# Attention probabilities of sixteen heads: TensorE transposes replaced by 32x32 squares on VectorE and a round trip through DRAM

## What is computed

```python
D_MODEL, SEQ, N_HEADS = 1024, 256, 16        # moba: 16 heads of 64
FOX_HEADS = MLA_HEADS = 8                    # odd: 8 heads of 64, 8 of 96
def moba_attention(h, w_qkv, w_o):
    ...
    s_own = jnp.einsum('bhqd,bhjd->bhqj', qc, ko).astype(jnp.float32)
    s_own = jnp.where(kpos[None, :] <= qpos[:, None], s_own, NEG_INF)
    p = jax.nn.softmax(jnp.concatenate([s_sel, s_own], axis=-1), axis=-1).astype(v.dtype)
    ...
def block_causal_attention(q, k, v, log_decay_cum):
    ...
        sc = jnp.einsum('bhqd,bhkd->bhqk', qi, k).astype(F32) * scale
        if fi is not None:
            sc = sc + fi[..., :, None] - log_decay_cum[:, :, None, :]
        sc = jnp.where(kpos[None, :] <= qpos[:, None], sc, -jnp.inf)
        p = jax.nn.softmax(sc, axis=-1).astype(v.dtype)
        return jnp.einsum('bhqk,bhkd->bhqd', p, v)
```

## Time and profile before

| | |
|---|---|
| median of 3 runs | 1202.47 us (1202.43 to 1202.48) |
| span of the profiled execution | 1201.0 us |
| TensorE busy | 1191.7 us (99%) |
| VectorE busy | 881.1 us (73%) |
| ScalarE busy | 661.8 us (55%) |
| GpSimd busy | 52.7 us (4%) |
| DMA moved | 217.80 MB, mean 181 GB/s |

### The profile page before, as it was taken

One profiled execution on the slowest core, in us unless ns is written; L12 is line 12 of the kernel. 1 busy time (PEld: TensorE's weight loads), 2 busy tenths in 40 slices (PEclk: granted clock), 3 DMA queues, 4 the chain that ended last, 5 costly groups with the idle time before them and its releaser, 6 DMA issues.

```text
span 1201.0 us, 16544 instructions
## 1 busy us (share of the span) xinstructions
PE 1191.7 (99%) x6611; PEld 1025.8 (85%) x6611; DVE 881.1 (73%) x1227; ACT 661.8 (55%) x871; POOL 52.7 (4%) x75
## 2 busy tenths in 40 slices
PE   9999999999999999999999999999999999999997
PEld 8888888888777888888899888888889977888886
DVE  6977989847786798884688877776467667777744
ACT  6545666634566666663587645444337775544430
POOL 0000000000000000000005200000012001000000
PEclk9999999999999999999999999999999999999999
DMA  9755555564534555556434556555526433755530
GB/s 359 248 206 192 174 179 192 187 221 170 195 114 138 188 180 179 203 201 216 160 102 141 185 211 236 191 195 191 179 91 229 176 140 106 253 202 175 198 119 35
DMA packets 32652, 217.80 MB, mean 181 GB/s; under 512 B 3760, under 2 KB 4032, under 8 KB 8000
## 3 DMA queue, kind: packets, MB, share of 16 engines
q1 hardware_dynamic: 30704, 210.39, 49.5%
q0 software_dynamic: 1728, 6.29, 1.6%
q10 hardware_dynamic: 144, 0.07, 0.0%
HBM read 215.67 MB, written 1.05 MB: 180 GB/s over the span
## 4 chain that ended last, share of the span: by engine, by line
PE 99%; DVE 1%; DMA 0%; ACT 0%; issue 0%
PE ps L963 43%; PE ps L893 24%; PE ps L899 14%; PE ps L901 4%; PE ps L915 2%; PE ps L912 2%; PE ps L911 2%; PE ps L1004 1%; PE ps L977 1%; PE ps L1032 1%; PE ps L1014 1%; PE ps L1096 1%; DMA t<-in_cst 0%; PE ps L1042 0%; PE ps L1081 0%; PE ps L926 0%
## 5 line engine op out<-in xcount | busy, mean ns | idle before, releaser
L963 PE MATMUL ps<-t,t 128*128 128x512 f32 (+3 forms) x2328 | 538.4, 387 | 0.0
L1552 DVE TENSOR_TENSOR t<-t,t 128x2048 fp32r<-128x2048 f32 (+3 forms) x200 | 448.8, 2257 | 101.9 <-PE ps L963 87.7
L963 PEld LDWEIGHTS ps<-t,t 128*128 128x128 f32 x2328 | 423.1, 188 | 81.5 <-issue 1.8
L1205 ACT CAST t<-t 128x2048 fp32r<-128x2048 f32 (+3 forms) x200 | 374.6, 1883 | 202.3 <-PE ps L963 106.0
L893 PE MATMUL ps<-t,t 128*128 128x512 f32 x1274 | 305.8, 390 | 0.0
L893 PEld LDWEIGHTS ps<-t,t 128*128 128x128 f32 x1274 | 238.9, 188 | 51.2
L899 PEld LDWEIGHTS ps<-t,t 128*128 128x128 f32 x1456 | 187.2, 191 | 7.4
L899 PE MATMUL ps<-t,t 128*128 128x256 f32 x1456 | 189.5, 283 | 0.0
L1687 DVE TENSOR_REDUCE t<-ps 128x512 f32<-128x1024 f32 x40 | 49.0, 1225 | 44.3 <-PE ps L901 44.3
L1640 DVE SCALAR_TENSOR_TENSOR t<-t,t,t 128x254 f32<-128x254 f32 (+1 forms) x176 | 73.2, 478 | 10.2 <-ACT t L1230 10.2
L1270 ACT CAST t<-t 128x512 fp32r<-128x512 f32 x44 | 27.3, 620 | 91.2 <-DVE t L1671 91.2
(11 more groups left out here) (220 smaller groups left out, 846.0 us busy)
## 6 DMA issues: line engine op xcount, KB each, us to landing
t<-in_wts SPq DMA_DIRECT2D x192, 1024.0 KB, 4.9
t<-in_rows POOLq DMA_DIRECT2D x12, 512.0 KB, 4.4
t<-in_wts SPq DMA_DIRECT2D x4, 528.0 KB, 4.1
t<-in_wts SPq DMA_DIRECT2D x2, 768.0 KB, 4.8
t<-in_wts SPq DMA_DIRECT2D x2, 592.0 KB, 3.8
t<-in_x_in SPq DMA_DIRECT2D x2, 512.0 KB, 4.3
out<-t SPq DMA_DIRECT2D x4, 256.0 KB, 2.0
t<-in_wts SPq DMA_DIRECT2D x2, 256.0 KB, 6.3
```

Source lines behind the costliest of these rows:

```text
L963: ins = mm(ps[:, t_bank(stage, t, j), 0:c1 - c0], a, w[:, k, c0:c1], start=kt == 0 and part == 0, stop=kt == KTS[stage] - 1 and part == 2)
L1205: copy(wh[:, k, 0:w], wraw[:, r, 0:w]).then_inc(s_hi, 1)
L1552: tt(wl[:, k, 0:w], wraw[:, r, 0:w], wh[:, h, 0:w].bitcast(F32), ALU.subtract).then_inc(s_lo, 1)
```

## The change

For heads 0 to 7 of moba and the eight fox heads (16 to 23) the step `u` is gone. In its place:

- `d`: VectorE transposes the scaled probabilities in 32x32 squares (one instruction of 128x384, `STREAM_TRANSPOSE`) into one of two buffers, and SyncE writes that buffer to a scratch in DRAM (`spilled_probs`), 1536 bytes per partition.
- `r`: SyncE waits for the write's landing (for heads 4 and up in the attention also for the values of the head four before) and reads the scratch back in 4x128 pieces of 384 bytes, into the buffer that the values step takes.

A square transpose alone leaves a key's number in the wrong partition. For these heads the keys are therefore stored in spread order (key 4r+b at place 32b+r), by the copies that bring them from PSUM, so that the read back lands each key in its own partition. The mask and the row of forget sums follow that order. The turned probabilities now lie as (query block of 32, chunk, query) for all 32 heads, so the values matmuls read them, and write PSUM, in pieces. TensorE waits for the reads of all heads of a values step. SyncE issues a load at `+l` instead of `+h`. Two values steps move: `p3` by three token steps, `p19` one ahead.

```diff
-@q1 t0.0 n1 t0.1 t1.0 +h t1.1 t2.0 +l +l vcopy0 t2.1 u0 s2 n2 u1 t3.0 t3.1 t4.0 n3 t4.1 t5.0 u2 s4 t5.1 u3 t6.0 t6.1
-n4 +h +l +h t7.0 t7.1
-@k1 t0.0 s6 n5 rope1.1.0 p3 t0.1 u4 t1.0 t1.1 t2.0 t2.1 t3.0 t3.1 u5 t4.0 n6 t4.1 t5.0 t5.1 +h +l u6 t6.0 t6.1 t7.0
-t7.1 cross1.1.0
+@q1 t0.0 n1 d1 r0 t0.1 t1.0 +h t1.1 t2.0 r1 +l +l vcopy0 t2.1 s2 n2 d2 t3.0 t3.1 t4.0 n3 d3 r2 t4.1 t5.0 s4 t5.1 t6.0
+r3 t6.1 n4 d4 +h +l +h t7.0 t7.1
+@k1 t0.0 s6 n5 d5 rope1.1.0 t0.1 t1.0 t1.1 p3 r4 t2.0 r5 t2.1 t3.0 t3.1 t4.0 n6 d6 t4.1 t5.0 t5.1 r6 +h +l t6.0 t6.1
+t7.0 t7.1 cross1.1.0
...
-+l +l +l t5.1 t6.0 +h +h vfcopy t6.1 n18 n19 t7.0 t7.1 f2.0 +l +h u17 f2.1 +l +h u18 qcopy1 f3.0 f3.1
-@uq kcopy1 u19 t0.0 s20 t1.0 s21 n20 t2.0 n21 +h s22 s23 queries0 t3.0 t0.1 p19 u20 n22 t1.1 t2.1 +h t3.1
++l +l +l t5.1 t6.0 +h +h vfcopy t6.1 n18 d18 r17 n19 d19 t7.0 t7.1 f2.0 r18 +l +h f2.1 r19 +l +h qcopy1 f3.0 f3.1
+@uq kcopy1 t0.0 s20 t1.0 s21 n20 d20 t2.0 n21 d21 +h s22 s23 queries0 t3.0 p19 r20 t0.1 n22 d22 r21 t1.1 t2.1 +h t3.1
...
+        def turn_squares(a, h):
+
+            n = D_AT[16 * a + h]
+            if n > 2:
+                dve.wait_ge(s_spill[(n - 1) % 2], 16 * ((n - 1) // 2))
+            dve.wait_ge(s_pnorm, 16 * a + h + 1)
+            dst = squares_of(16 * a + h).rearrange("p (b c i) -> p c b i", b=4, c=3)
+            nc.vector.transpose(dst, ATT_MEM[a][0][:, h % 4, :].rearrange("p (c b i) -> p c b i", c=3, b=4)
+                                ).then_inc(s_square, 1)
...
-            if kind in ("pump", "pump_hi"):
+            if kind in ("pump", "pump_lo"):
...
+            elif kind == "d":
+                n = D_AT[k[0]]
+                sp.wait_ge(s_square, n)
+                dma(spill[n - 1], squares_of(k[0])).then_inc(s_spill[(n - 1) % 2], 16)
+            elif kind == "r":
+                a, h = k[0] // 16, k[0] % 16
+                n = D_AT[k[0]]
+                sp.wait_ge(*spilled(k[0]))
+                if h >= 4:
+                    sp.wait_ge(s_pv, valued_at(16 * a + h - 4))
+                dma(ATT_MEM[a][1][:, h % 4, :].rearrange("p (a f) -> p a f", a=4),
+                    spill[n - 1].rearrange("q f -> (q f)").rearrange("(a p f) -> p a f", a=4, p=128)
+                    ).then_inc(s_back[h % 4], 16)
...
-            pe.wait_ge(s_ptc, 16 * a + last + 1)
+            for i in range(first, last + 1):
+                way, n = probs_left(16 * a + i)
+                if way == "u":
+                    pe.wait_ge(s_ptc, n)
+                else:
+                    pe.wait_ge(*back(16 * a + i))
...
-                        ins = mm(ps[64 * (i % 2):64 * (i % 2) + 64, 7, n * S + q.start:n * S + q.stop],
-                                 value_of(a, i, kt), PT[:, i % 4, p], start=kt == 0, stop=kt == 1)
+                        o = ps[64 * (i % 2):64 * (i % 2) + 64, 7, n * S + q.start:n * S + q.stop]
+                        ins = mm(o.rearrange("p (c a i) -> p a c i", a=4, i=32), value_of(a, i, kt),
+                                 turned_probs(a, i)[:, :, c, :], start=kt == 0, stop=kt == 1)
...
+                if is_k:
+                    for i in range(4):
+                        ins = copy(spread_keys(kh[0:64, 4 * m + i, :]),
+                                   in_spread_order(s3[64 * (i % 2):64 * (i % 2) + 64, i // 2, :]))
+                    ins.then_inc(s_kc, 1)
+                    return
```

More of the change, by code:

```diff
@@ L115 @@
 for _name, _cols in (("uo", 256), ("gt", 128), ("mask", 256), ("rope", 128), ("rope2", 64), ("cnt", 64),
[L116 removed]
+                     ("ident", 128), ("gain", 8), ("spread_mask", 256)):
     CST[_name] = _n
@@ L317, in all_steps @@
     out += [("rows", 2)] + ffn_steps(0, 2)
-    out += [("rows", 3), ] + mixed_steps(MOBA, None, 3)
+    out += [("rows", 3), ("probs_mask", 1)] + mixed_steps(MOBA, None, 3)
     out += [("rows", 4)] + ffn_steps(1, 4)
@@ L321, in all_steps @@
     out += [("rows", 6)] + ffn_steps(2, 6)
-    out += mixed_steps(ODD, "odd", 7)
+    out += [("probs_mask", 3)] + mixed_steps(ODD, "odd", 7)
     out += [("rows", 8)] + ffn_steps(3, 8)
@@ L358, with probs_left @@
 VALUED = [s[1] for s in STEPS if s[0] == "p"]
+U_AT = {s[1]: n for s, n in counted("u").items()}
+D_AT = {s[1]: n for s, n in counted("d").items()}
+SPREAD = set(range(8)) | set(range(16, 24))
+def probs_left(h):
+    return ("d", D_AT[h]) if h in D_AT else ("u", U_AT[h])
 def valued_from(last):
@@ L437, in program @@
     brow = fixed.take([128, 1024])
-    cs = fixed.take([128, NCST])
+    cs = fixed.take([128, NFIX])
     vecs = fixed.take([128, NVEC])
@@ L518, in program @@
     fc, fc2 = early.take([8, S]), early.take([8, S])
+    odd_squares = area_at(area.at).take([128, 2, 384])
     vm, vf = area.take([128, 2, 512]), area.take([128, 2, 512])
@@ L561, in program @@
     s_oh, s_ol = sem("s_heads_hi"), sem("s_heads_lo")
+    s_smask, s_square = sem("s_spread_mask_loaded"), sem("s_probs_squares_turned")
+    s_spill = [sem("s_even_probs_spilled"), sem("s_odd_probs_spilled")]
+    s_back = [sem(f"s_probs{i}_back") for i in range(4)]
     s_pw, s_us, s_xtap = sem("s_pool_w_loaded"), sem("s_u_copied"), sem("s_x_tap")
@@ L826, in six_free @@
         if was[0] == "u":
-            return s_ptc, was[1] + 1
+            return s_ptc, U_AT[was[1]]
         return (s_ac, ACROSS_AT[was]) if a else (s_crossed, CROSS_AT[was])
@@ L846, in qk_of, with squares_of, turned_probs, spilled @@
         return (qmT if is_q else kmT)[:, h - 8, cols]
+    SPREAD_MASK = (moba_mask, odd_mask)
+    def squares_of(h):
+        return (moba_squares if h < 16 else odd_squares if h < 20 else late_squares)[:, D_AT[h] % 2, :]
+    def turned_probs(a, h):
+        return ATT_MEM[a][1][:, h % 4, :].rearrange("p (a c i) -> p a c i", a=4, c=3)
+    def spilled(h):
+        n = D_AT[h]
+        return s_spill[(n - 1) % 2], 16 * ((n + 1) // 2)
+    def back(h):
+        return s_back[h % 4], 16 * sum(d <= h and d % 4 == h % 4 for d in D_AT)
+    def in_spread_order(ap):
+        return ap.rearrange("p (n r b) -> p n b r", r=32, b=4)
+    def spread_keys(ap):
+        return ap.rearrange("p (n b r) -> p n b r", b=4, r=32)
     def att_scale(a, h):
@@ L1017, in values @@
         def values(a, last):
-            PT, first = ATT_MEM[a][1], valued_from(16 * a + last) - 16 * a
+            first = valued_from(16 * a + last) - 16 * a
             if first:
@@ L1295, in copy_cross @@
                 copy(qT[:, i1:i1 + 2, :], s3).then_inc(s_crossed, 1)
+            elif 2 * i1 in SPREAD:
+                keys = kT[:, i1:i1 + 2, :].rearrange("p a s -> p (a s)")
+                copy(spread_keys(keys), in_spread_order(ps[:, 6, :])).then_inc(s_crossed, 1)
             else:
@@ L1422, in odd_step @@
                 act.wait_ge(s_t, T_AT["t", "ukv", 1, t])
+                for h in (18, 19):
+                    act.wait_ge(*spilled(h))
                 b2 = ps[:, 2 * t:2 * t + 2, :]
@@ L1431, in odd_step @@
                 act.wait_ge(s_acm, ACROSS_AT["across", a, i])
+                if a:
+                    for h in (22, 23):
+                        act.wait_ge(*spilled(h))
                 copy((kmT if a else qmT)[:, 2 * i:2 * i + 2, :].rearrange("p a b -> p (a b)"),
@@ L1694, in maxima @@
                 dve.wait_ge(s_pnorm, H - 3)
-                dve.wait_ge(s_pt, H - 3)
-            for sl, masked, col in ((slice(0, 128), MASK[:, 128:256], 0), (slice(128, 384), MASK, 1)):
+                way, n = probs_left(H - 4)
+                dve.wait_ge(*((s_pt, n) if way == "u" else (s_square, n)))
+            mask = MASK
+            if H in SPREAD:
+                dve.wait_ge(s_smask, 16 * (a + 1))
+                mask = SPREAD_MASK[a]
+            for sl, masked, col in ((slice(0, 128), mask[:, 128:256], 0), (slice(128, 384), mask[:, 0:256], 1)):
                 ins = nc.vector.tensor_tensor_reduce(
```

40 lines of the change are left out of this document (27 added, 13 removed).

## The result

| | before | after |
|---|---|---|
| median | 1202.49 us (18 runs, 1202.32 to 1203.60) | 1204.92 us (18 runs, 1202.37 to 1206.68) |
| ratio to before | | 1.0019, 95% interval 1.0012 to 1.0025 |
| span of the profiled execution | 1201.0 us | 1203.5 us |

The change makes the kernel slightly slower, by about 0.2%; the forecast was 1197.8, the range ended at 1203.0. The runs of after also scatter over 4 us, where most of those before agree within 0.3.

The account below looks back on a forecast made before the run. TensorE, busy 99% of the span, was taken to bound the kernel. 1202.5 minus 5.5 for turns, plus 0.4 for fox keys and 0.4 for the round trip, gave 1197.8 us, range 1196.5 to 1203.0.

Parts of the forecast that it names:

- Turns removed: TensorE: 48 of 96 transposes go, 11 turns at 0.36 us and 5 at 0.30, saving 5.5 us.
- Values matmuls in pieces: TensorE's values matmuls, reading in pieces, 64 also writing PSUM in runs of 32 columns: cost 0, at worst +16.5 us.
- The second rival: Values matmuls pay for the pieces, making the kernel slower: 1208.0 us if the 64 writing in runs double; chance 0.10.
- Squares: VectorE's 16 new transposes of 384 numbers take 0.55 us each, hidden by idleness behind heads 0 and 1: cost 0.
- Fox keys: Four key copies replace two; scores of head 20 wait 0.4 us more, bounds 0 and 1.3.
- The round trip: Scratch write and read: 1.5 us margin before values of heads 0 to 3, 0.4 us wait before those of 16 to 19.
- The prediction's own sign of being wrong: Among its signs: over 1 us of waiting for the scratch before any values step.
- The third rival: Probabilities come back late, write and read each 1 or 2 us longer: 1200.3 or 1204.3 us; chance 0.15, time 1201.
- The held loads: SyncE's weight loads go out 1 to 4 us late but are early enough for ScalarE's rounding: cost 0.
- The fifth rival: TensorE meets its feeders sooner, and the 5.5 us return as waits at stage ends: 1202.3 us; chance 0.08.

Follow-up runs that it names:

- version 10: Changed kernel with one weight load issued later, the second of the pair in stage q1, behind head 3's read; 1202.95 us, ratio 1.0005.
- version 7: Changed kernel with only three of SyncE's weight loads issued later, behind scratch writes or reads; 1200.01 us, ratio 0.9983.
- version 9: Changed kernel with three weight loads issued later as in version 7, plus five reorderings for VectorE and ScalarE; 1197.37 us, ratio 0.9957.
- version 2: Changed kernel without the trip: squares go straight into the buffer the values step reads, 32 scratch DMAs left out; 1200.52 us, ratio 0.9982.
- version 5: Changed kernel with both later values steps (heads 0 to 3, 16 to 19) and four buffers for squares of heads 0 to 7; 1204.33 us, ratio 1.0015.
- version 3: Changed kernel with four buffers instead of two for the squares of heads 0 to 7; 1204.59 us, ratio 1.0008.
- version 4: Changed kernel with values of heads 0 to 3 five token steps later and of 16 to 19 two later; 1204.99 us, ratio 1.0020.
- version 6: As version 5, plus reordering rotations, scores of head 20 and the first across step against waits on VectorE and ScalarE; 1202.07 us, ratio 0.9995.

## Why the prediction was wrong, by its own steps

- **Turns removed, 5.5 us.** Right: 48 instead of 96, and the version in which no new wait is left is 5.1 us shorter in span (1195.9) and in median.
- **Values matmuls in pieces, 0.** Right: 396 and 273 ns against 397 and 273. The ends of matmuls are modelled in a profile, but the starts say the same: from the first of sixteen to the next weight matmul 1.45 us before (335.82 to 337.27) and after (339.94 to 341.39). The second rival falls. The Trainium skill's sentence (PSUM — Partial Sum Buffer, Specifications) on non-contiguous patterns does not show here: runs of 32 columns cost nothing that the trace can tell.
- **Squares, 0.55 us each, hidden.** Size right (0.579), cover wrong. I checked the cover only behind heads 0 and 1. Behind the squares of heads 4 to 7, 16 and 22 VectorE makes rotations and maxima for which TensorE did not wait before; now they come later, and TensorE, without its turns, earlier. Even without a trip 0.8, 0.8 and 0.3 us of waits came from it.
- **Fox keys, 0.4 us.** Four copies take 1.50 us as worked out. The scores of head 20 began at 952.19 where six matmuls from 950.34, at the 1.28 of before, give 951.62: 0.57. The 0.12 that I counted as room was the delay from the copies' end to the scores; after, it is 0.15 (952.04 to 952.19).
- **The round trip: a margin of 1.5 us at heads 0 to 3, and a wait of 0.4 at 16 to 19.** The failed step. I took the landing of the second load of a pair, 6.5 us, and set it at 324.8 + 6.5. In the trace both loads went out at 325.1 and 325.6, since SyncE stood waiting for head 1's write, itself behind the load at 316.4, before it could read and then load. They landed 7.3 and 9.6 us after issue. The second followed the first by 0.6 us instead of the 2.2 of before, and the first was itself slow, as version 10's single load is behind the same two reads. So head 2's write landed at 335.7, not 332.0, and the margin of 1.5 became a wait of 3.0. At heads 16 to 19 the stage as a whole ran 1.8 us later than before (the same scores at 930.77 and 929.00). With that taken off, the third load landed at 951.2 instead of 949.6, head 19's read at 958.1 instead of 955.8, and TensorE was ready at 956.3 instead of 955.4: a wait of 1.96 instead of 0.4. I had the order right (a write lands behind the loads) and took loads for unaffected by the waits and the reads that the change itself puts ahead of them. The prediction's own sign of being wrong came: over 1 us of waiting for the scratch before a values step.
- **The third rival** (probabilities late, up to 1204.3, chance 0.15) named the time by luck, with the wrong reason: it priced small pieces in the trip itself. With nothing ahead a write lands in 1.9 us and a read in 2.4 to 2.8 (version 7 and the changed kernel). What the reads do cost, they cost the loads behind them.
- **VectorE's buffer, not in the sum.** The square of head 4 waits for head 2's write, 3.65 us, and with it weight subtractions and rotations. I named what waits on SyncE and not what waits on VectorE.
- **The held loads, 0.** Right as far as it went: rounding waited 15.7 us for loads instead of 12.5, and no TensorE wait came of it.
- **The fifth rival** (freed time is no time, chance 0.08) holds for half: against version 9, 2.6 to 3.2 of the 5.1 us had come back in versions 7 and 2, 2.0 and 2.5 of them as waits for VectorE and ScalarE, and by order alone they could be taken away.

The ledger of the changed kernel, in us: 5.1 saved; 3.0 and 1.96 lost at the scratch; 1.0 at the crossing (9.28 from 341.39 to 350.67, where version 9 takes 8.29 for the same 36 matmuls), 0.57 at scores 20, 0.3 at scores 19: 1.7 longer, where the profiled spans differ by 2.5. Of the other 0.8, 0.3 lies at the program's start (8.12 against 7.78 in version 9); the rest is not traced.

## What to carry to other kernels

A small DMA whose landing an engine waits for must be costed with the bytes that are already on their way, on every queue, and with the waits that it puts on the engine that issues those; issue bulk loads that have time to spare behind it. When work goes off the bounding engine, look at each engine's order between the new work and the next thing that the bounding engine needs of it, not only at idle time where the new work stands. A wait that moves when its consumer is moved has its cause upstream: here two such moves gave nothing, and three loads issued later gave 4.9 us. And look at the granted clock behind every long wait of the bounding engine: behind one of 4.2 us it fell here and cost 1.5 us more, which no list of waits shows.

## What the runs showed of the hardware

- A write of 192 KB from GpSimd's queue with three 1 MB loads of SyncE's ahead landed with the last of them, 7.6 us after its issue. The Trainium skill (DMA: Bandwidth & Descriptors, Issuing engines are not separate DMA queues) says that DMAs of all issuing engines run on the same 16 DMA engines and interleave. That they share them agrees with the trace, since the write was held by loads of another queue. That they interleave shows too, but late. From 944 to 948, with this write issued at 944.1, only SyncE's queue moved packets (1.42 MB); from 948 to 950 both did:

```profile
q1 hardware_dynamic: 190, 1.42, 99.9%
...
q1 hardware_dynamic: 59, 0.39, 49.6%
q0 software_dynamic: 107, 0.37, 45.1%
```

What held the write's packets for 4 us is not shown.
- With nothing ahead, a write of 192 KB landed in 1.9 us and a read in 384-byte pieces in 2.4 to 2.8. On SyncE's queue a write behind loads landed 0.3 to 2.5 us after the last of them, mostly within 1.1: 4.7 us after issue behind one load in the changed kernel (at 319.3; 3.1 in version 10), 7.4 behind two (at 328.3; 5.1 in version 7 at 941.5), 8.3 behind three (at 944.9).
- A 1 MB load with nothing under way landed in 4.7 to 5.4 us; with two of these reads issued within about 1 us ahead of it, in 7.3 to 8.2 (ten loads).
- Behind waits of TensorE of 3.4, 3.6 and 4.2 us (versions 5, 3 and 4) the granted clock fell from 2.4 to 1.2 GHz for some 3 us; behind those of 2.9 us (the changed kernel) and 2.1 (version 6) it did not.
- A transpose in 32x32 squares of 128x384 float32 takes 579 ns on VectorE, and matmuls of 256 columns with moving operand and PSUM in runs of 32 (396 ns against 397) take no longer than in one run.
